# Key-query weights kept in idle tiles across both token tiles, and a new cost table for spreading gather slots, in a diffusion backbone with retrieved experts

## What is computed

```python
h = rmsnorm(x, norm_attn_g[l]) * (1 + sc1) + sh1          # hc likewise for the context
y, yc = parallel_mixers(h, hc, p, ...)                     # w_in, two head groups, w_out
x = x + g1 * y
h = rmsnorm(x, norm_ffn_g[l]) * (1 + sc2) + sh2
x = x + g2 * peer_ffn(h, p)                                # context too, unless last

def expert_block(xb):                                      # peer_ffn, 128 tokens
    q = (xb @ p['peer_wq']).reshape(128, 8, 2, 128)        # key queries, 8 heads
    s = jnp.einsum('thcd,ckd->thck', q, p['peer_subkeys'])
    ...                                                    # top 16 of 16 x 16 pairs per head
    u, v = peer_u[eidx], peer_v[eidx]                      # 128 experts per token
    act = gelu(jnp.einsum('ted,td->te', u, xb)) * gate
    return jnp.einsum('te,ted->td', act, v)
```

## Time and profile before

| what | value |
|---|---|
| median of 3 runs | 2603.52 us |
| profiled execution | 2593.61 us, its span 2591.8 us |
| busy, share of span | PE 80%, DVE 71%, ACT 44%, POOL 37% |
| moved by DMA | 980.25 MB, 378 GB/s over the span |
| HBM read | 977.62 MB |
| first and last dot of a slot | about 221 us and 2580 us |

### The profile page before, as it was taken

One profiled execution on the slowest core, in us unless ns is written; L12 is line 12 of the kernel. 1 busy time (PEld: TensorE's weight loads), 2 busy tenths in 40 slices (PEclk: granted clock), 3 DMA queues, 4 the chain that ended last, 5 costly groups with the idle time before them and its releaser, 6 DMA issues.

```text
span 2591.8 us, 26277 instructions
## 1 busy us (share of the span) xinstructions
PE 2062.6 (80%) x6968; PEld 1092.8 (42%) x6968; DVE 1835.4 (71%) x4200; ACT 1145.3 (44%) x3145; POOL 963.5 (37%) x909
## 2 busy tenths in 40 slices
PE   6996788778979876987777797888787887677766
PEld 2554444444435444444334343444453444333322
DVE  0247986996667779976979556683596787867776
ACT  2123474444337444734433624553244644433333
POOL 0013344333433433554343343340133343344553
PEclk8998898889999988999888899998988998788988
DMA  9588999999998999999999999998699999999997
GB/s 355 198 284 329 402 396 397 406 379 355 415 395 357 393 394 381 416 417 411 414 416 367 345 396 403 399 396 308 254 408 371 382 411 395 414 381 420 421 419 329
DMA packets 215704, 980.25 MB, mean 378 GB/s; under 512 B 17660, under 2 KB 75544, under 8 KB 117272
## 3 DMA queue, kind: packets, MB, share of 16 engines
q0 software_dynamic: 121744, 848.35, 80.7%
q1 hardware_dynamic: 91640, 122.00, 13.6%
q10 hardware_dynamic: 2192, 8.39, 0.8%
HBM read 977.62 MB, written 1.05 MB: 378 GB/s over the span
## 4 chain that ended last, share of the span: by engine, by line
PE 33%; DVE 27%; DMA 21%; ACT 10%; issue 8%; POOL 1%; POOLq 0%; ACTq 0%; DVEq 0%; SPq 0%
DMA EXPERT<-in_peer_uv,FIX 19%; PE VS L1141 13%; PE PA L910 11%; DVE EXPERT L1888 9%; DVE ACC L1898 3%; DVE SCR L1435 2%; PE PA L938 2%; PE PB L831 2%; DMA EXPERT<-in_w_ada 1%; ACT L1374 1%; PE VS L863 1%; ACT DIAG L1389 1%; ACT WEI L1384 1%; PE PB L1131 1%; DVE SI L1840 1%
## 5 line engine op out<-in xcount | busy, mean ns | idle before, releaser
L1141 PE MATMUL VS<-EXPERT,DIAG 128*128 128x512 f32 x2304 | 1168.8, 649 | 243.1 <-ACT DIAG L1389 242.8
L742 POOL DMA_INDIRECT EXPERT<-in_peer_uv,FIX x768 | 896.0, 1167 | 1106.8 <-PE VS L1141 758.0
L1888 DVE CUSTOM_DVE_ANT_0 EXPERT<-EXPERT,H 128x1024 f32<-128x1024 f32 x768 | 923.1, 1224 | 309.5 <-DMA EXPERT<-in_peer_uv,FIX 300.6
L1141 PEld LDWEIGHTS VS<-EXPERT,DIAG 128*128 128x128 f32 x2304 | 455.6, 208 | 817.4 <-issue 462.8
L1382 ACT ACTIVATE GEL<-DOT 128x1 f32<-128x1 f32 x768 | 155.0, 202 | 1018.9 <-DVE DOT L1888 1017.5
L910 PE MATMUL PA<-WT,HT 128*128 128x512 f32 (+2 forms) x720 | 296.1, 557 | 7.6 <-issue 4.4
L1898 DVE SCALAR_TENSOR_TENSOR ACC<-EXPERT,WEI,ACC 128x1024 f32<-128x1024 f32 x192 | 246.2, 1282 | 31.1 <-ACT WEI L1384 31.1
L1389 ACT ACTIVATE DIAG<-IDN,WEI 128x128 f32<-128x128 f32 x576 | 231.3, 402 | 68.2 <-PE VS L1141 50.4
L1384 ACT ACTIVATE WEI<-GEL,GATE 128x1 f32<-128x1 f32 x768 | 226.3, 295 | 24.9
L1131 PE MATMUL PB<-HT,WT 128*128 128x128 f32 (+1 forms) x1472 | 212.3, 305 | 28.6 <-issue 27.4
L1131 PEld LDWEIGHTS PB<-HT,WT 128*128 128x128 f32 x1472 | 205.5, 216 | 53.6 <-issue 51.2
(11 more groups left out here) (194 smaller groups left out, 1721.3 us busy)
## 6 DMA issues: line engine op xcount, KB each, us to landing
WT<-in_peer_wq SPq DMA_DIRECT2D x92, 512.0 KB, 17.2
EXPERT<-in_w_ada POOLq DMA_DIRECT2D x41, 1024.0 KB, 10.7
WT<-in_w_in SPq DMA_DIRECT2D x48, 512.0 KB, 8.5
WT<-in_w_out SPq DMA_DIRECT2D x48, 512.0 KB, 10.4
EXPERT<-in_peer_uv,FIX POOLq DMA_INDIRECT x768, 11.3
EXPERT<-in_w_ada ACTq DMA_DIRECT2D x7, 1024.0 KB, 13.1
WT<-in_w_in SPq DMA_DIRECT2D x16, 384.0 KB, 8.1
WT<-in_w_in SPq DMA_DIRECT2D x16, 288.0 KB, 5.6
```

Of the source, the lines that this page charges most:

```text
L742: pool.indirect_dma_start(out=EXPERT[:, j, :], out_offset=None, in_=a["peer_uv"], in_offset=bass.IndirectOffsetOnAxis(ap=FIX[:, par, j:j + ...
L1141: ins = nc.tensor.matmul(VSUM[n][:, :], DIAG[:, i, :], EXPERT[:, j, D + n * W:D + (n + 1) * W], start=first, stop=last_one)
L1888: nc.vector.tensor_tensor_reduce(out=EXPERT[:, j, 0:D], in0=EXPERT[:, j, 0:D], in1=H2[:, b % HB, :], scale=1.0, scalar=0.0, op0=ALU.mult, ...
```

## The change

Four heads of peer_wq of layer 0 (4 to 7) are loaded once for the context, in eight DMAs placed between the w_in pieces "kd" and "vd" of the prelude, into tiles that hold nothing until the latent front: the halves of KTM, KTD, VM and VD for tiles 2 and 3, H2 block 2, X tiles 2 and 3. Both passes (tile 0, then tile 1) read them there. X's latent tiles are therefore loaded later, after the last read, a step of tile 1's picks; SP waits there for `stay_used`. The order of tile 1's heads becomes 4, 5, 6, 7, 0, 1, 2, 3. In layer 1 head 7 of the latent group is loaded once, in two DMAs in the gap between the layers, into X tile 1 and H2 block 0. The pieces that these heads had in WT go away (92 become 72, plus 10 resident loads). And the costs by which slots are spread change.

```diff
+STAYS = {(0, CTX): (4, 5, 6, 7), (1, LAT): (7,)}
+FIRST = {(0, CTX): 4, (0, LAT): ALONE[0, LAT], (1, LAT): 0}
 def order_of(l, g, t):
-    n = 0 if t == 0 else ALONE[l, g]
+    n = 0 if t == 0 else FIRST[l, g]
     return [*range(n, PH), *range(n)]
...
-COST = {... "in": (0, 20), "up": (0, 25), "attn": (50, 0), "out": (0, 22) ...}
+PIECE = {"in": 20, "up": 25, "out": 20}
+MAPS = {CTX: 30, LAT: 60}
 def cost(s):
+    if s[0] in PIECE:
+        return PIECE[s[0]] * len(s[PER_TILE[s[0]]])
+    if s[0] == "attn":
+        return MAPS[s[2]]
...
-        KTM = sb("KTM", [MQ, MH, TILES * P])
+        KTMW = sb("KTM", [P, MH, TILES * P])
+        KTM = KTMW[0:MQ, :, :]
+        HOME = {(0, CTX): [KTMW[:, 0:4, 2 * P:4 * P], KTMW[:, 4:8, 2 * P:4 * P], KTD[:, :, 2 * P:4 * P], four(VM[:, 2:4, :]),
+                           four(VD[:, 2:4, :]), four(H2[:, 2:3, :]), four(X[:, 2:3, :]), four(X[:, 3:4, :])],
+                (1, LAT): [four(X[:, 1:2, :]), four(H2[:, 0:1, :])]}
...
-            elif kind == "pick" and stage[4]:
+            elif kind == "pick" and stage[4] and not stays(stage):
...
+        X_LAT_AFTER = ("pick", 0, CTX, (2, (1,), 0), (3, (1,), 1))
+        STAY_LAST = ("more", 0, CTX, (6, (1,), 0), (7, (1,), 1))
...
+                if stage[:3] == ("in", 0, CTX) and stage[3] in ("kd", "vd"):
+                    stay(0, CTX, PARTS * ("kd", "vd").index(stage[3]) + stage[5])
+                if stage == X_LAT_AFTER:
+                    sp.wait_ge(stay_used, 1)
                     for t in range(2, TILES):
                         sp.dma_start(X[:, t, :], ...).then_inc(x_in[LAT], 16)
+                if stage == ("in", 1, LAT, "vd", (1,), PARTS - 1):
+                    sp.wait_ge(x_ready[3], 4)
+                    for half in range(2):
+                        stay(1, LAT, half)
...
+                    if stays(stage):
+                        pe.wait_ge(stay_in[l, g], 32 * len(STAYS[l, g]))
+                        held["w"] = [head_home(l, g, cur[0], half) for half in range(2)]
```

More of the change, by code:

```diff
@@ L154, with stays @@
 ALONE = {(0, CTX): PH, (0, LAT): 6, (1, LAT): PH}
+STAYS = {(0, CTX): (4, 5, 6, 7), (1, LAT): (7,)}
+FIRST = {(0, CTX): 4, (0, LAT): ALONE[0, LAT], (1, LAT): 0}
 def order_of(l, g, t):
-    n = 0 if t == 0 else ALONE[l, g]
+    n = 0 if t == 0 else FIRST[l, g]
     return [*range(n, PH), *range(n)]
+def stays(s):
+    return s[4] is not None and s[4][0] in STAYS.get((s[1], s[2]), ())
 def pick(l, g, heads):
@@ L182, in pick_apart @@
     return (pick(l, g, [(h, (0,)) for h in range(n)]),
-            pick(l, g, [(h, BOTH) for h in range(n, PH)] + [(h, (1,)) for h in range(n)]))
+            pick(l, g, [(h, BOTH if h >= n else (1,)) for h in order_of(l, g, 1)]))
 def holds(s):
@@ L227, in mingle @@
     return out + second[at:]
-COST = {"stat": (45, 0), "norm": (50, 0), "in": (0, 20), "turn": (0, 10), "root": (5, 5), "up": (0, 25), "attn": (50, 0), "early": (50, 0),
-        "hnorm": (20, 0), "heads": (20, 0), "gates": (10, 0), "rows": (10, 0), "out": (0, 22), "back": (20, 0), "pick": (45, 0), "more": (40, 0), "also": (45, 0), "then": (40, 0),
+COST = {"stat": (45, 0), "norm": (50, 0), "in": (0, 0), "turn": (0, 10), "root": (5, 5), "up": (0, 0), "attn": (50, 0), "early": (50, 0),
+        "hnorm": (20, 0), "heads": (20, 0), "gates": (10, 0), "rows": (10, 0), "out": (0, 0), "back": (20, 0), "pick": (45, 0), "more": (40, 0), "also": (45, 0), "then": (40, 0),
         "ada": (18, 0), "adae": (4, 0), "adat": (10, 0), "mod": (5, 0)}
+PIECE = {"in": 20, "up": 25, "out": 20}
+MAPS = {CTX: 30, LAT: 60}
 PER_TILE = {"in": 4, "turn": 4, "root": 4, "up": 4, "out": 4}
 def cost(s):
+    if s[0] in PIECE:
+        return PIECE[s[0]] * len(s[PER_TILE[s[0]]])
+    if s[0] == "attn":
+        return MAPS[s[2]]
     each, per_tile = COST[s[0]]
@@ L593, in backbone, with four, head_home @@
         QP = SCR[:, 3072:4096].rearrange("p (r c n) -> p r c n", r=2, c=2)
+        def four(tile):
+            return tile.rearrange("p t n -> p (t n)").rearrange("p (k n) -> p k n", k=HP)
+        HOME = {(0, CTX): [KTMW[:, 0:4, 2 * P:4 * P], KTMW[:, 4:8, 2 * P:4 * P], KTD[:, :, 2 * P:4 * P], four(VM[:, 2:4, :]),
+                           four(VD[:, 2:4, :]), four(H2[:, 2:3, :]), four(X[:, 2:3, :]), four(X[:, 3:4, :])],
+                (1, LAT): [four(X[:, 1:2, :]), four(H2[:, 0:1, :])]}
+        def head_home(l, g, h, half):
+            return HOME[l, g][2 * STAYS[l, g].index(h) + half]
         def ht(k, t):
@@ L605, in backbone @@
         fg_in = sem("fg_in")
+        stay_in, stay_used = {at: sem(f"stay_in{at[0]}") for at in STAYS}, sem("stay_used")
         piece_in = [sem(f"piece_in{i}") for i in range(WSLOTS)]
@@ L691, in _, with stay @@
             sp.wait_ge(first_in[5], 16)
+            def stay(l, g, n):
+                v, h = a["peer_wq"][l].rearrange("(k p) n -> p k n", p=P), STAYS[l, g][n // 2]
+                k = n % 2 * HP
+                sp.dma_start(HOME[l, g][n], v[:, k:k + HP, h * HW:(h + 1) * HW]).then_inc(stay_in[l, g], 16)
             n = 0
@@ L702, in _ @@
                     n += 1
-                if stage == ("out", 0, CTX, 0, (0,), 0):
+                if stage[:3] == ("in", 0, CTX) and stage[3] in ("kd", "vd"):
+                    stay(0, CTX, PARTS * ("kd", "vd").index(stage[3]) + stage[5])
+                if stage == X_LAT_AFTER:
+                    sp.wait_ge(stay_used, 1)
                     for t in range(2, TILES):
                         sp.dma_start(X[:, t, :], a["x"][0, (t - 2) * P:(t - 1) * P, :]).then_inc(x_in[LAT], 16)
+                if stage == ("in", 1, LAT, "vd", (1,), PARTS - 1):
+                    sp.wait_ge(x_ready[3], 4)
+                    for half in range(2):
+                        stay(1, LAT, half)
                 if stage == ("close", 4):
@@ L796, in _ @@
             owed = []
+            held = {}
             def release():
+                if "stay" in held:
+                    pe.wait_ge(filled_b, held.pop("stay"))
+                    pe.sem_inc(stay_used, 1)
                 while owed:
@@ L1113, in pick_ @@
                 if cur is not None:
-                    held["w"] = [head_piece() for k in range(0, KD, HP)]
+                    if stays(stage):
+                        pe.wait_ge(stay_in[l, g], 32 * len(STAYS[l, g]))
+                        held["w"] = [head_home(l, g, cur[0], half) for half in range(2)]
+                    else:
+                        held["w"] = [head_piece() for k in range(0, KD, HP)]
                     key_query(cur, 0, prev is None)
@@ L1120, in more @@
                     key_query(cur, 1)
-                    owed.append((filled_b, rb.n, KD // HP))
+                    if not stays(stage):
+                        owed.append((filled_b, rb.n, KD // HP))
+                    elif stage == STAY_LAST:
+                        held["stay"] = rb.n
             def key_query(cur, c, first=False):
```

## The result

The change is slightly slower: 2603.22 us median of 20 runs (2598.45 to 2609.35) against 2594.18 us of 20 runs of the kernel before (2584.01 to 2605.51), ratio 1.003 with a 95% interval of 1.0018 to 1.0042. I had forecast 2578.5 us, a gain of 25.0 us on the 2603.52 us of the first three runs. Those three lay high in the kernel's spread; against the 20 runs the change costs 9.0 us, so the forecast of the difference is off by 34 us. The profiled executions lie as far apart as the medians: spans of 2591.8 and 2600.5 us.

The account below looks back on a forecast made before the run. Transfers were taken to set the pace of the slots, VectorE close behind in the picks. -11.3 - 7.1 - 2.6 - 3.0 - 3.0 + 2.0 = -25.0 us: profiled 2593.61 to 2568.6, median 2578.5; range 2567 to 2599.

Parts of the forecast that it names:

- The first picks and the second picks: Layer 0, context picks: fewer weight pieces shorten them to VectorE's need, 95 to 91.2 us and 132 to 125.0 us.
- The context attention: Layer 0, context tile 1: with ten slots fewer it shrinks from 78 us to 56.4 us; 65 us the bad end.
- w_out of context 1: Layer 0, one slot more: 42.8 us by VectorE; DMA's 47.6 covered by a ring left full by earlier stages.
- The stages 221 to 571: Layer 0, four context stages: 315.4 us for 350; nine slots moved later cost 23.3, net -11.3 us.
- Seven slots for the latent attention of tile 0, -7.1: Layer 0, at 776 us: idle DMA there takes part of seven added slots, 100.0 us against 107.1.
- its five more and all other exchanges are even: Latent attention at 1031 us, DMA share already 1.01: its five added slots, and other slot moves, gain or lose nothing.
- the five slots of the attention there: Layer 1, latent attention at 2020 us, DMA share 0.97: five added slots make 98.3 us against 100.9, -2.6 us.
- Layer 1's weights: Layer 1, two pieces less in latent tile 0's picks and two in the last 425 us: -3.0 us each.
- What was added: Resident loads in the prelude and in the gap between layers: +1.0 us each, each between 0 and 3.
- the +3 of a doubled price: Prelude: by a skill page's queue rule resident loads count double, three taking 9 us against 5.9 slack: +3, not +1.
- The second: Rival, chance 0.20: context attention needs 60 to 65 us, latent attentions gain nothing; about -11 us, 2592.5.
- The fourth: Rival, chance 0.05: buffer returns set the pace, removed pieces shorten no stage, resident loads paid in full; +15.1 us, 2618.6.

Follow-up runs that it names:

- the weights alone: The whole change with the cost table of before, so every stage keeps its old slots, against the kernel before: 2592.61 us, ratio 0.9997 (0.9982 to 1.0013).

## Why the prediction was wrong

The first picks and the second picks. The step that failed is "I take for each the larger of what is left of DMA work and what VectorE needs (the window less its waits for gathers)". I put 91.2 and 125.0 us; the weights alone gave 94.0 and 131.5, the whole change 93.9 and 129.6. The error is in what the waits for gathers are. I took them for bandwidth; they stay when the DMA share falls from 1.02 to 0.94. So of 10.8 us counted in these two stages nothing measurable came with the old slots. The waits lie in the first 23 us of the stage, and the heads after them run at VectorE's own speed, which four heads' worth of the window would have shown me before: 96% busy and not one wait. With it falls the sentence that the step rests on, "So transfers set the pace of the slots": equal GB/s in unlike stages didn't show it. I had read an average over a stage as one limit.

The context attention. I put 56.4 us; it took 60.3 with the weights and 59.2 without. The slots gave back 1.9 us each where I had 2.2; a size, not a mechanism, though what holds the stage at 60 us was not tested.

w_out of context 1 took 46.1 us where I had 42.8, near the 47.6 that DMA alone would make. VectorE's waits for gathers there, in the window 376:422 of the kernel after, grew from 3.8 us, so the ring carried nothing that counts:

```profile
DVE EXPERT L1944 <- DMA EXPERT<-in_peer_uv,FIX: 5.4, 6, 2.0
```

The stages 221 to 571 took 329.9 us from dot to dot where I had 315.4, and against 349.3 before, nine slots at 2.59 (23.3 us) make that +3.9 instead of -11.3. This is the larger error, 15 us.

The exchanges. Seven slots for the latent attention of tile 0, -7.1, was right, in the mechanism too. I had 7.1 us of idle DMA there, 2.7 slots' worth, and the full price after them; three slots cost next to nothing there and the next four 2.4 us each. At 1.4 us a slot on average the exchange is 7 x (2.59 - 1.4) = 8.3 us. The step "its five more and all other exchanges are even" was near the truth in layer 0: from the latent front to slot 400 the nine slots more cost 20 us where I had 16.2. There slots that go into the latent front cost 3.3 us each (four profiles with 69 slots, mean 211.9 us, four with 67, mean 205.4) and those into the latent attention of tile 1 about 3.4 (120 for 103 us), and w_out of that tile gave back 3.2 for each of its three. The step failed in layer 1: from slot 512 on the table costs 8.4 us where I had -2.6, and the five slots of the attention there, which I took for a gain, paid their full price. I had looked at the DMA share of the stages that get slots, and not at what covers the short stages that lose them.

Layer 1's weights. First picks -3.0: 0.0 measured, the same mistake as in the context picks, there with a DMA share of 1.02 too. Last picks -3.0: some -2.6, right; there VectorE is at 73%.

What was added. +1.0 for the prelude and +1.0 for the gap: the first dot moved by 0.2 us and TensorE waited 0.85 us. Right, and the +3 of a doubled price wasn't seen: in the kernel after TensorE was busy for all of 40 to 80 us. X's latent tiles came in time: issued at 508.33 us, first read at 560.43, and ScalarE waited for none.

The errors add up to 32 of the 34 us: 15.2 in the stages from 221 to 571 us, 4 in the rest of layer 0, 11.0 for layer 1's table, 3.4 for its weights, less 1.0 for prelude and gap.

Of the rivals, none is what happened. The second had the right direction, compute paying more for each slot, and was too mild: it still had 6 us of gain in the picks. The fourth came nearest, +15.1 us for +9.0, but with a false mechanism: the prelude took its loads for nothing, loads added in the picks cost 10.5 us, and in the last 425 us two pieces less did pay. That rival's first half, "20 pieces less shorten latency and no stage", is true of the 18 outside the last picks as long as the slots stay where they are.

## What to carry to other kernels

A DMA share of 1.0 and an engine at 92% can lie close together as limits of the same stage: here a load added cost more than its DMA time and a load removed nothing, until other work moved in. So after freeing a resource, move work into the stage that was freed, in the same change, and price a moved slot by what it costs where it goes and where it leaves, each read from the stage's length in profiles with different counts. A wait for a transfer is not a measure of what bandwidth is worth: look whether it lies in the steady part of the stage or at its start.

And when a table of costs spreads filler work over a program, look for the longest run of dependent steps that it leaves without any. Here the one pause that grew from 11 to 17 us stood in VectorE's list before anything ran.

## What the runs showed of the hardware that I had not expected

DMA engines can read full for 130 us (share 1.01 to 1.03, about 400 GB/s) without setting the length of that stage: with 0.92 to 0.94 and 350 to 374 GB/s the same heads took the same time to 0.4 us in 51. And six more loads of 512 KB on SP's queue did not show up in the gathers' waits at all (7.3 for 7.0 us), but in three waits of TensorE before matmuls whose weights come by the same queue, 20.0 us together. All three kernels in which such a wait reaches 7 us in these picks (eight loads added, six loads added, 41 slots without resident weights; 16.0, 20.0 and 12.1 us) have their extra time in one or two pauses beside it, and not in every head.
